# First projection on the input before its norm, modulation slices between projections, decayed keys and queries one head later

## The chip, the cores and the metric

One core of one Trainium2 chip runs the whole program. The time is the device time of that core in microseconds (us); the kernel before takes 1657.59 us, the median of three runs (1657.0 to 1659.45). All arithmetic is in 32-bit floats. TensorE is called PE, VectorE DVE, ScalarE ACT, GpSimd POOL, and the queue that issues the loads SP.

## What is computed

Two transformer blocks on one sequence of 256 tokens with 1024 features. Only the parts that the change touches stand here.

```python
# block 1
h = rms_norm(x, norm_mix_g)          # x * rsqrt(mean(x*x)) * g
u = h @ w_in                         # q, k, v; conv input a, b; state space input
sb, conv, ssm = attention(..), conformer_conv(..), s5_ssm(..)
x = x + branch_norm(concat(sb, conv, ssm)) @ w_out
x = x + memory_cross_attention(rms_norm(x), rms_norm(mem), ..)
x = x + ffn(rms_norm(x))
# block 2
mod   = silu(c) @ w_mod_2 + b_mod_2             # six rows of 1024: shifts, scales, gains
mod_c = silu(c_ctx) @ w_mod_2 + b_mod_2
h, hc = modulated norms of x and ctx
y = mLSTM(h, hc) and gated linear attention(h, hc), then w_out_2
x = x + g1 * y
x = x + g2 * peer_ffn(..)            # 16384 experts, read densely
return rms_norm_2(x, norm_f_g)
```

In gated linear attention the keys and queries are multiplied by exponentials of a running sum of the log decays ("decayed keys", "decayed queries") before the scores `att`.

## The kernel before

Activations lie feature-major: 8 tiles of 128 features by 256 tokens, `x[:, k, :]`. Five engines run five instruction lists, written out by hand; semaphores join them. What stands earlier on an engine's list runs earlier, and a wait on a list holds up all that stands behind it.

**Weights** come in slices of 1 MB into a ring of six slots. PE's list sets the order of the slices (`weights()`), and SP issues the loads in that order (L1178), each when PE has finished with the slice six places before it. One projection (`project`, 16 matmuls of 128x128 by 256 tokens) uses one slice, and so does one step of `mod_items`, which does only four matmuls with a 32-column stationary operand.

**Products** go round four PSUM banks (`begin`), and a bank is written again only after the engine that takes its product has read it. Some later products use four upper banks (`upper=1`).

**Start.** ACT squares x, PE sums the squares over the features (`mix_sum`), ACT takes the square root, DVE the reciprocal (L1255), and DVE then writes h = x * g * r in eight slices (L1278), each released on its own. PE runs three projections from it: "u" (slice 8 of `w_in`), "conv_b" and "conv_a". DVE does a long run of small state space work after h, up to b_ready, then copies u (L1326), subtracts the turns (L1329), takes conv_a (L1333), normalizes the memory tokens and runs the 31 taps of the convolution (L1346). PE waits for the taps later on.

**Modulation.** The product with `w_mod` is cut into 24 slices, eight for each of three rows, which lie between other work. The function `mod_items(n)` does n of them. After eight, ACT copies a row (`mod_row`, L2073), and `mod_turn(r)` turns it on PE. Before the change 4, 2 and 5 slices stand close together just ahead of the first output projection ("mix_out", 0 to 3); seven are earlier, six later. The mixed activations are ready after three norms in a row on DVE (state space, convolution, attention; L1255 and L1457).

**Gated linear attention** lies between the four heads of mLSTM. PE's list is `similarities(0)`, ..., `similarities(3)`, `values(2)`, `values_of("gv", 2)`, the four transposes of the decayed keys and the scores (`gla_keys_and_scores`), `values_of("gv", 3)`, `values(3)`, then the sums "add" and the gates "mo" and "gr". DVE's list, head by head, is `latent_decays(hd+1)` (L1750), `decayed(hd+1)` (L1759), then `quotient(hd)` (L1774 to L1785), and at head 1 `decayed_keys()` (L1729) ahead of the quotient and `decayed_queries()` (L1737 to L1739) behind it. Two bank rules matter: the second product of `similarities(3)` goes to a bank that `quotient(1)` has to clear, and the first of `values(2)` to one that `latent_decays(3)` has to clear.

## Time and profile before

| what | value |
|---|---|
| median of three runs | 1657.59 us |
| the profiled execution | 1655.44 us, span 1652.2 us |
| PE busy | 1585.1 us, 96% of the span |
| PE weight loads busy | 1423.3 us, 86% |
| DVE busy | 1114.6 us, 67% |
| ACT busy | 719.7 us, 44% |
| the chain that ended last | PE 87%, DVE 8%, DMA 3%, ACT 1% |
| mean granted clock of TensorE | 0.98 of full speed |

The span is the time from the first to the last instruction of the profiled execution. All moments below are us from its start. The chain that ended last is followed backwards from the last instruction: a share of an engine in it is time in which nothing else would have let the program end sooner. PE's idle time is what the change can reach; it lies mostly in the first 350 us and between 640 and 790 us. A PE matmul of 32-bit floats shows as two entries, so "x16" is eight matmuls.

### The profile page before, as it was taken

To read this page: it belongs to the slowest core of one execution; us is meant where nothing else is said; L and a number is where in the kernel's file an instruction comes from. 1 tells how busy PE (TensorE), PEld (TensorE's weight loads), DVE (VectorE), ACT (ScalarE), POOL (GpSimd) and SP (SyncE) were. 2 spreads that over 40 slices of the span, in tenths; PEclk is the share of its full clock that TensorE was granted. 3 is DMA by queue.
4 is the path that set the end of the run, shared out by engine and by line. 5 is a ranking of instruction groups with operands and counts; after the bars stand their busy time and mean duration, and the time that the engine had idled before them with its cause. 6 is when DMAs were issued, how large, how long until landed. Compare 5 with 4: busy or idle time off the path is not lost.

```text
span 1652.2 us, 28703 instructions
## 1 busy us (share of the span) xinstructions
PE 1585.1 (96%) x10694; PEld 1423.3 (86%) x10694; DVE 1114.6 (67%) x1943; ACT 719.7 (44%) x1034; POOL 53.8 (3%) x104
## 2 busy tenths in 40 slices
PE   7999899899999999899999999999999999999996
PEld 6677477689999988688999999999999888888885
DVE  6993231347544696675559999898894777777776
ACT  4225201344443456242444565555554544444442
POOL 2001000000000003400000000000000000000000
PEclk9999899999999999999899999999999999999998
DMA  6253834535553323061538887755557777777773
GB/s 264 102 195 131 370 114 178 180 115 188 180 179 104 108 77 103 1 221 62 189 89 229 223 226 226 216 155 161 160 149 223 231 236 237 238 237 236 237 235 103
DMA packets 94400, 293.59 MB, mean 178 GB/s; under 512 B 10480, under 2 KB 43376, under 8 KB 81392
## 3 DMA queue, kind: packets, MB, share of 16 engines
q1 hardware_dynamic: 94176, 292.21, 54.7%
q8 instruction: 57, 0.93, 0.2%
q14 instruction: 23, 0.19, 0.0%
q10 hardware_dynamic: 144, 0.26, 0.0%
HBM read 274.60 MB, written 17.83 MB: 177 GB/s over the span
## 4 chain that ended last, share of the span: by engine, by line
PE 87%; DVE 8%; DMA 3%; ACT 1%; issue 1%; SPq 0%; DVEq 0%; POOL 0%; ACTq 0%
PE ps L428 87%; DMA ring<-in_w_mod 1%; DVE big L1346 1%; DVE split_ring L1880 1%; DVE big L1776 1%; DVE big L1255 1%; DMA ring<-in_peer_u 0%; DVE hh L1556 0%; DVE x L2015 0%; DMA ring<-in_w_mo 0%; DVE big L1929 0%; DVE big L1933 0%; DVE big L1931 0%; DMA ring<-in_w_gv 0%; DMA kept_acts<-par 0%
## 5 line engine op out<-in xcount | busy, mean ns | idle before, releaser
L428 PE MATMUL ps<-split_hh,split_ring 128*128 128x256 f32 x3296 | 410.3, 284 | 3.2 <-DVE split_ring L1880 2.0
L428 PEld LDWEIGHTS ps<-split_hh,split_ring 128*128 128x128 f32 x3296 | 400.4, 192 | 4.6 <-ACT big L2040 1.4
L428 PE MATMUL ps<-split_ring 128*128 128x256 f32 (+1 forms) x2224 | 391.0, 335 | 2.2 <-DVE split_ring L1880 2.1
L428 PEld LDWEIGHTS ps<-split_ring 128*128 128x128 f32 x2224 | 339.1, 188 | 47.6 <-DVE split_ring L1880 2.4
L1880 DVE TENSOR_TENSOR split_ring<-ring,split_ring 128x1024 fp32r<-128x1024 f32 x256 | 311.6, 1219 | 49.5 <-ACT split_ring L2415 46.2
L2422 ACT ACTIVATE split_ring<-ring 128x1024 fp32r<-128x1024 f32 x128 | 135.9, 1062 | 179.2 <-DMA ring<-in_peer_v 179.2
L2415 ACT ACTIVATE split_ring<-ring 128x1024 fp32r<-128x1024 f32 x128 | 135.2, 1057 | 63.4 <-DMA ring<-in_peer_u 63.4
L428 PE MATMUL ps<-split_ffn_h,split_ffn_w 128*128 128x256 f32 x1056 | 130.4, 287 | 3.5 <-ACT split_ffn_h L2236 3.5
L428 PEld LDWEIGHTS ps<-split_ffn_h,split_ffn_w 128*128 128x128 f32 x1056 | 129.3, 194 | 4.6 <-issue 3.9
L1527 DVE TENSOR_TENSOR split_ffn_w<-ring,split_ffn_w 128x2048 fp32r<-128x2048 f32 x33 | 75.6, 2290 | 54.7 <-ACT split_ffn_w L2221 54.7
L428 PE MATMUL ps<-hh,ring 128*128 128x256 f32 x480 | 107.8, 386 | 4.3 <-DVE hh L1278 4.3
L1989 DVE TENSOR_TENSOR split_ring<-ring,split_ring 128x256 fp32r<-128x256 f32 x128 | 54.4, 425 | 84.9 <-ACT split_ring L2429 84.8
L428 PEld LDWEIGHTS ps<-hh,ring 128*128 128x128 f32 x480 | 92.6, 194 | 19.7 <-issue 6.9
L428 PE MATMUL ps<-big 128*128 128x256 f32 (+12 forms) x656 | 88.6, 327 | 14.1 <-DVE big L1750 4.8
L428 PEld LDWEIGHTS ps<-big 128*128 128x128 f32 (+5 forms) x656 | 69.9, 169 | 36.7 <-issue 17.2
L2040 ACT ACTIVATE big<-ps 128x512 f32<-128x512 f32 (+1 forms) x62 | 35.2, 595 | 147.9 <-PE ps L428 124.9
L428 PE MATMUL ps<-big,ring 128*128 128x256 f32 x408 | 92.1, 386 | 0.8 <-DVE big L1515 0.8
L428 PEld LDWEIGHTS ps<-big,ring 128*128 128x128 f32 x408 | 78.5, 194 | 13.4 <-issue 1.4
L1984 DVE TENSOR_TENSOR ring<-ring,big 128x256 f32<-128x256 f32 x128 | 80.3, 628 | 1.5 <-DMA ring<-kept_acts 1.4
L2221 ACT ACTIVATE split_ffn_w<-ring 128x2048 fp32r<-128x2048 f32 x33 | 63.0, 1909 | 32.3 <-PE ps L428 32.3
L1963 DVE TENSOR_SCALAR ring<-tables,idx 128x128 f32<-128x128 f32 x256 | 71.1, 341 | 6.2 <-PE ps L428 6.2
L428 PE MATMUL ps<-split_hid_high,split_ffn_w 128*128 128x256 f32 x352 | 63.5, 283 | 0.0
(312 smaller groups left out, 1779.4 us busy)
## 6 DMA issues: line engine op xcount, KB each, us to landing
ring<-in_peer_u SPq DMA_DIRECT2D x128, 512.0 KB, 3.9
ring<-in_peer_v SPq DMA_DIRECT2D x128, 512.0 KB, 3.6
ring<-in_w_mod SPq DMA_DIRECT2D x24, 1024.0 KB, 5.2
ring<-in_ffn_in SPq DMA_DIRECT2D x22, 1024.0 KB, 4.9
ring<-kept_acts SPq DMA_DIRECT2D x128, 128.0 KB, 3.4
ring<-in_ffn_out SPq DMA_DIRECT2D x11, 1024.0 KB, 4.9
ring<-in_w_out SPq DMA_DIRECT2D x8, 1024.0 KB, 11.8
ring<-in_peer_wq SPq DMA_DIRECT2D x8, 1024.0 KB, 6.4
```

What stands on the lines that cost most here:

```text
L428: return nc.tensor.matmul(out, lhsT, rhs, start=start, stop=stop, skip_group_check=True)
L1255: link(v.reciprocal(r, r))
L1346: ins = v.scalar_tensor_tensor(conv[:, a, :], src, w, conv[:, a, :], ALU.mult, ALU.add)
L1527: v.tensor_tensor(fw_low[:, q, :], ring[:, (ffn_at + n) % RING, :], fw_high[:, q, :].bitcast(F32), ALU.subtract).then_inc(flag("ffn_weight ...
L1880: v.tensor_tensor(low[:, q, :], tile[:, q, :], high[q].bitcast(F32), ALU.subtract)\
L1963: v.tensor_scalar(hot[n % 4][:, q, 0, :], iota, idx[:, 0, at:at + 1], idx[:, 2, at:at + 1], ALU.is_equal, ALU.mult)
L1984: v.tensor_tensor(weighted_[:, q, :], act_in[:, q, :], g_, ALU.mult).then_inc(flag("whole_weighted"), 1)
L1989: v.tensor_tensor(w_low[:, q, :], weighted_[:, q, :], w_high[:, q, :].bitcast(F32), ALU.subtract).then_inc(e_ready, 1)
L2040: s.took(key, a_(dst, bank if src is None else src(bank), ACT.Copy, scale=scale))
L2221: a_(fw_high[:, n % 3, :], ring[:, at % RING, :], ACT.Copy).then_inc(flag("ffn_weights_high"), 1)
L2415: a_(u_high[q], u_tile[:, q, :], ACT.Copy).then_inc(flag("u_high_ready"), 1)
L2422: a_(v_high[q], v_tile[:, q, :], ACT.Copy).then_inc(flag("v_high_ready"), 1)
```

## The change

It has three parts.

1. **First projection.** DVE writes xg = x * g in eight slices while the sum of squares is still being taken, and PE projects "u" from xg. The factor r, which is one number for each token, is multiplied in when DVE takes the product. The slices of h are written as before, and "conv_b" is now the first to use them.
2. **Modulation slices.** The groups of 4, 2 and 5 ahead of "mix_out" become 2 and 2. Of the other seven, three follow the first three projections of "mix_out", one stands ahead of the first projection of "xq", two follow its first two and one follows its sums. The second turn moves to that last place, and ACT's copy of the second row goes between its takings of "xq".
3. **Decayed keys and queries.** On DVE they move from head 1 to head 2, together with the low half of weight half 21. On PE the fourth block of values, "gv" 3, goes between the transposes of the keys and the scores, and ACT copies it out ahead of the scores.

```diff
@@ tensor
-            project("u", ("dve",), "w_in", 8, arriving("h_mix"))
-            project("conv_b", ("act",), "w_in", 7, hk)
+            def scaled(k):
+                pe.wait_ge(flag("x_scaled"), k + 1)
+                return xg[:, k, :]
+            project("u", ("dve",), "w_in", 8, scaled)
+            project("conv_b", ("act",), "w_in", 7, arriving("h_mix"))
...
-            mod_items(4)
             weighted(3)
             mod_items(2)
-            mod_turn(0)
             pe.wait_ge(flag("branch_squares_ready"), 3)
             total("sb_sum", [sq[:, i, :] for i in range(4)])
-            mod_items(5)
-            mod_turn(1)
+            mod_items(2)
+            mod_turn(0)
             pe.wait_ge(flag("mixed_ready"), 3)
             for i in range(4):
                 project(("mix_out", i), ("dve",), "w_out", i, lambda k: mixed[:, k, :])
+                if i < 3:
+                    mod_items(1)
...
+            mod_items(1)
             arrived = arriving("h_xa")
             for i in range(4):
                 project(("xq", i), ("act",), "xa_wq", i, arrived)
+                if i < 2:
+                    mod_items(1)
             pe.wait_ge(flag("squares_ready"), 4)
             sums_of_heads("xq_sum")
+            mod_items(1)
+            mod_turn(1)
             inverses_of_heads("xq", 0)
...
             values_of("gv", 2, wv, 1)
-            gla_keys_and_scores()
+            gla_keys()
             values_of("gv", 3, wv, 1)
             release_half(*wv)
+            gla_scores()
             values(3)
@@ vector
-            r = reciprocal_std("mix_sum")
-            for i in range(4):
-                s.wait(f"x_loaded{i}", 16)
+            for k in range(KD):
+                s.wait(f"x_loaded{k // 2}", 16)
+                v.tensor_scalar(xg[:, k, :], x[:, k, :], col("mix_g", k), None, ALU.mult).then_inc(flag("x_scaled"), 1)
+            mix_r = r = reciprocal_std("mix_sum")
...
-            s.took("u", v.tensor_copy(u.rearrange("p a t -> p (a t)"), bank))
+            s.took("u", v.tensor_tensor(u, bank.rearrange("p (a t) -> p a t", a=2),
+                                        mix_r.unsqueeze(1).broadcast_to([P, 2, T]), ALU.mult))
...
-                if hd == 1:
+                if hd == 2:
                     decayed_keys()
                 quotient(hd)
-                if hd == 1:
+                if hd == 2:
                     decayed_queries()
                     half_low(21)
@@ scalar
             squares(sq, xk).then_inc(flag("squares_ready"), 1)
-            mod_row(1)
...
             for i in range(4):
                 heads_raw("xq", i, xq)
+                if i == 2:
+                    mod_row(1)
...
+            copy_out(("gv", 3), gv[:, 3, :])
             s.wait("att_zeroed")
...
-            copy_out(("gv", 3), gv[:, 3, :])
```

The buffer of xg is that of `mixed`, which is written only much later.

**PE around the modulation slices.** A row with `ps<-ring,big 32x512` is the slices (x4 is one slice), `128x8` a turn, `big,ones` a sum over features, and `big,ring 128x256` the "mix_out" projections (x16 is one). Before:

```order
L428 MATMUL ps<-big,ones 128x256 x4
L428 MATMUL ps<-ring,big 32x512 x16
L428 MATMUL ps<-big 64x256
L428 MATMUL ps<-big 64x128
L428 MATMUL ps<-big 64x256
L428 MATMUL ps<-big 64x128
L428 MATMUL ps<-ring,big 32x512 x8
L428 MATMUL ps<-big 128x8 x4
L428 MATMUL ps<-big,ones 128x256 x4
L428 MATMUL ps<-ring,big 32x512 x20
L428 MATMUL ps<-big 128x8 x4
L428 MATMUL ps<-big,ring 128x256 x32
```

The same place in the changed kernel, from the last attention pair on:

```order
L429 MATMUL ps<-ring,big 32x512 x8
L429 MATMUL ps<-big,ones 128x256 x4
L429 MATMUL ps<-ring,big 32x512 x8
L429 MATMUL ps<-big 128x8 x4
L429 MATMUL ps<-big,ring 128x256 x16
L429 MATMUL ps<-ring,big 32x512 x4
L429 MATMUL ps<-big,ring 128x256 x16
L429 MATMUL ps<-ring,big 32x512 x4
L429 MATMUL ps<-big,ones 32x256 x8
L429 MATMUL ps<-big,ring 128x256 x16
L429 MATMUL ps<-ring,big 32x512 x4
```

Four slices stand ahead of the first output projection in place of eleven, and one behind each of the first three.

**DVE at heads 1 and 2 of gated linear attention.** Before, from the end of `decayed(2)`: the keys are L1729, the quotient of head 1 L1774 to L1785, the queries begin with L1737.

```order
L1759 SCALAR_TENSOR_TENSOR big<-ps,big 128x256
L1729 TENSOR_TENSOR big<-big 128x1024 x2
L1774 SCALAR_TENSOR_TENSOR big<-ps,big 128x256
L1775 TENSOR_TENSOR big<-big,ps 128x256
L1776 RECIPROCAL big<-big 128x256
L1778 TENSOR_TENSOR big<-ps,big 128x256
L1774 SCALAR_TENSOR_TENSOR big<-ps,big 128x256
L1775 TENSOR_TENSOR big<-big,ps 128x256
L1776 RECIPROCAL big<-big 128x256
L1782 TENSOR_TENSOR big<-ps,big 128x256
L1785 TENSOR_TENSOR big<-big 128x256
L1737 TENSOR_TENSOR big<-big 128x512
```

In the changed kernel, from the end of the quotient of head 1 (L1801): L1766 is `latent_decays(3)`, L1775 `decayed(3)`, and L1745 the keys.

```order
L1798 TENSOR_TENSOR big<-ps,big 128x256
L1801 TENSOR_TENSOR big<-big 128x256
L1766 TENSOR_SCALAR big<-ps,big 128x256
L1766 TENSOR_SCALAR big<-ps,big 128x128 x2
L1766 TENSOR_SCALAR big<-ps,big 128x256
L1775 SCALAR_TENSOR_TENSOR big<-ps,big 128x512 x2
L1775 SCALAR_TENSOR_TENSOR big<-ps,big 128x256
L1775 SCALAR_TENSOR_TENSOR big<-ps,big 128x128 x2
L1775 SCALAR_TENSOR_TENSOR big<-ps,big 128x256
L1745 TENSOR_TENSOR big<-big 128x1024 x2
```

The quotient of head 1 now follows `decayed(2)` directly, and the decays of head 3 follow it, ahead of the keys.

## Rows read from the trace of the kernel before

**Rows 1.** The page: the chain that ended last, by engine

```profile
PE 87%; DVE 8%; DMA 3%; ACT 1%; issue 1%; SPq 0%; DVEq 0%; POOL 0%; ACTq 0%
```

**Rows 2.** The timeline of the start (start us, duration us, engine, line, operation, count [idle before, releaser])

```profile
5.76 6.34 PE L428 MATMUL ps<-big,ones 128*128 128x256 f32 x16 [5.76 <-ACT big L2031]
...
7.14 0.70 DVE L1272 MEMSET big<- 128x768 f32 x1
...
15.78 3.26 DVE L1278 SCALAR_TENSOR_TENSOR hh<-x,par,big 128x256 f32<-128x256 f32 x8
...
16.41 16.50 PE L428 MATMUL ps<-hh,ring 128*128 128x256 f32 x64 [4.31 <-DVE hh L1278]
...
32.84 4.49 DVE L1329 TENSOR_TENSOR big<-big 128x2048 f32<-128x2048 f32 x2
...
36.20 7.07 PE L428 MATMUL ps<-hh,ring 128*128 128x256 f32 x32
...
43.38 0.69 DVE L1333 TENSOR_TENSOR big<-ps,big 128x512 f32<-128x512 f32 x1 [6.04 <-PE ps L428]
```

**Rows 3.** DMA issues between 3.1 and 3.5 us: count, size, us to landing

```profile
ring<-in_w_in SPq DMA_DIRECT2D x1, 1024.0 KB, 7.6
```

**Rows 4.** Windows: us, busy PE, PEld, DVE, ACT, POOL (x instructions), PEclk, DMA share, GB/s

```profile
16.40:20.00 3.60, 3.59 (x9) 2.88 (x10) 3.43 (x13) 3.57 (x7) 0.00 (x0) 0.50 1.01 423
282.00:286.00 4.00, 4.00 (x10) 3.11 (x11) 1.89 (x5) 0.00 (x0) 0.00 (x0) 0.50 0.43 180
```

**Rows 5.** Waits of PE for the slices: us in total, times, longest

```profile
PE ps L428 <- DMA ring<-in_w_mod: 6.9, 7, 1.4
```

**Rows 6.** The timeline, 170 to 200 us: slices, norms, first output projection

```profile
173.10 2.78 PE L428 MATMUL ps<-ring,big 128*32 128x512 f32 x24
...
174.79 1.75 DVE L1255 RECIPROCAL big<-big 128x256 f32<-128x256 f32 x1 [3.70 <-ACT big L2036]
...
176.12 1.07 PE L428 MATMUL ps<-ring,big 128*32 128x512 f32 x8 [0.24 <-DMA ring<-in_w_mod]
...
187.37 1.67 DVE L1457 SCALAR_TENSOR_TENSOR big<-big,par 128x256 f32<-128x256 f32 x4
...
192.22 1.94 PE L428 MATMUL ps<-ring,big 128*32 128x512 f32 x8 [1.44 <-DMA ring<-in_w_mod]
...
198.29 16.02 PE L428 MATMUL ps<-big,ring 128*128 128x256 f32 x64
```

**Rows 7.** The timeline after the "xq" projections

```profile
281.95 3.78 PE L428 MATMUL ps<-big,tables 128*128 128x256 f32 x8 [2.41 <-DVE big L1469]
```

**Rows 8.** DVE, 664 to 684 us

```profile
665.03 3.20 DVE L1729 TENSOR_TENSOR big<-big 128x1024 f32<-128x1024 f32 x2
...
674.80 0.68 DVE L1737 TENSOR_TENSOR big<-big 128x512 f32<-128x512 f32 x1
...
678.41 1.21 DVE L1596 TENSOR_TENSOR split_ring<-ring,split_ring 128x1024 fp32r<-128x1024 f32 x1
...
682.33 2.34 DVE L1759 SCALAR_TENSOR_TENSOR big<-ps,big 128x512 f32<-128x512 f32 x6 [1.40 <-POOL big L2576]
```

**Rows 9.** ACT, exponentials of head 3 (second direction)

```profile
675.28 0.83 ACT L2321 ACTIVATE big<-ps,big 128x256 f32<-128x256 f32 x2
```

**Rows 10.** PE, 674 to 716 us

```profile
674.48 1.13 PE L428 MATMUL ps<-big 128*128 128x256 f32 x4 [1.81 <-DVE big L1782]
680.43 3.29 PE L428 MATMUL ps<-big 128*128 128x256 f32 x8 [4.82 <-DVE big L1750]
...
693.27 2.69 PE L428 MATMUL ps<-big 64*64 64x64 f32 x64
...
701.46 1.68 PE L428 MATMUL ps<-big 128*128 128x256 f32 x8
...
705.45 1.59 PE L428 MATMUL ps<-big 64*64 64x128 f32 x32
...
715.36 1.09 PE L428 MATMUL ps<-big 64*64 64x128 f32 x16 [1.34 <-DVE big L1782]
```

More of the change, by code:

```diff
@@ L197, in program @@
         mixed = area.take(8, T)
+        xg = mixed
         mod_rows = area.take(2, 512)
@@ L917, in values, with gla_keys @@
                     last.then_inc(made, 1)
-            def gla_keys_and_scores():
+            def gla_keys():
                 pe.wait_ge(flag("gla_ready"), 1)
@@ L926, in gla_keys_and_scores, with gla_scores @@
                     last.then_inc(made, 1)
+            def gla_scores():
                 pe.wait_ge(flag("gla_ready"), 2)
```

## The prediction

> **What bounds the kernel now.** I read the chain that ended last first: 87% of the span is PE and only 8% DVE and 3% DMA [rows 1]. So the end moves only where PE idles or runs at the low clock, and the first question for each part is how much of either lies at its place. Then I read the timeline at the three places the change touches, with the granted clock of TensorE from the windows. A change within 0.2% (3.3 us) is about what a measurement of this kernel cannot tell from none.
>
> At the start PE ends the sum of squares at 5.76 + 6.34 = 12.1 us and then waits 4.31 us for the first slice of h [rows 2]. The clock is 0.50 of full speed, the 1.2 GHz level, when PE comes back [rows 4]. The next 64 entries take 16.50 us, where 32 entries of the same kind take 7.07 us later, so 64 at full speed take 14.1 and 2.4 us are lost.
>
> Ahead of "mix_out" PE waits seven times for slices, 6.9 us in total [rows 5]. The slices cost 2.78 us for 24 entries, 0.93 us each, and 1.94 us at the low clock [rows 6]. "mix_out" starts at 198.29, 9 us after the last norm is ready (187.37 + 1.67 = 189.0), and its first 64 entries take 16.02 in place of 14.1 us. After "xq" PE waits 2.41 us for a reciprocal and then runs at the low clock again [rows 4, 7].
>
> In gated linear attention PE waits 1.81, 4.82 and 1.34 us for DVE, and the eight entries after the second wait take 3.29 us, where the same eight take 1.68 us later [rows 10].
>
> **Part 1, the first projection.** DVE is free at 7.14 + 0.70 = 7.84. Eight slices of xg at 0.41 us, the price of a slice of h (3.26 for eight), are done at 11.2 [rows 2]. A simpler operation may be cheaper; either way they end before 12.1 and before the square root that the reciprocal needs, so they cost nothing. The weights were issued at 3.1 and landed 7.6 us later, 10.7 [rows 3]. So "u" starts at 12.1 with no gap behind the sum, and I take full speed. "u" ends at 19.2; h is complete at 15.78 + 3.26 = 19.0, so "conv_b" has no wait. It ends at 26.3. The memory sum (36.20 - 32.91 = 3.3) and "conv_a" (7.07) end at 36.7. DVE, whose list up to there is not moved, is done with the turns at 32.84 + 4.49 = 37.3 [rows 2]. It then takes "conv_a" at 37.4 and not at 43.38: **6.0 us** earlier. The taps hang on that and PE waits for the taps, so 6.0 is what counts, not the 6.7 that PE gains. Taking "u" is now a product with r; the like operation on "conv_a" from PSUM takes 0.69 us [rows 2] and lies ahead of b_t on PE by several us. If only the wait goes and not the clock loss, the gain is 4.3.
>
> **Part 2, the slices.** Times here are on the old axis. The last attention pair goes first, 0.9 us from 173.1, then two slices to 175.9, the attention sum 0.9 and two slices to about 178.8; the fourth slice of this place landed by 176.12 in the old order [rows 6], so none waits. With the turn (0.9) PE is through at 179.8. The norms are DVE's: from 174.79 it does three reciprocals of 1.75 and eight products (0.42 each from 1.67 for four) [rows 6], 8.7 us in all, so the mixed activations are ready at 183.5. "mix_out" starts there and not at 198.29: 14.8 us. PE now has a new wait of 3.7 us. Behind it come six slices (5.6 us) that were ahead of it, and the 1.9 us at the low clock in "mix_out" may go: 14.8 + 1.9 - 5.6 = 11.1. The seventh slice and the second turn (1.9 us) fill the wait of 2.41 us after "xq" [rows 7] and cost nothing; without that wait they would cost 1.9. What was half speed behind it (4.00 us busy in 282 to 286 at 0.50 [rows 4], and 1.2 us more) costs 2.6 us that I take as saved. Against it stands the new wait of 3.7 us, of a length with the 4.31 us after which the clock was low at the start; I charge 2.0 us in "mix_out", near the 1.9 and 2.4 us lost there in the rows, with 0 and 3.4 as ends. Part 2 gives **11.7 us**, with 6 and 13.7 as ends. SP: each moved slice issues one load of 1 MB. Before, eleven came with next to no PE work between them; now 1 MB of slice and 1 MB of weights go with 8 us of PE work, and in the saturated stretch of the start (423 GB/s [rows 4]) 2 MB take 5 us. ACT's copy of the second row (0.6 us) lies between two takings that are 7 us apart.
>
> The Trainium skill (TensorE: Matmul & The Clock Gate, Part 1) says that the throttled state is the default, that activity releases it, and that the cold stretch of one and the same kernel differs from run to run, so one should not fit to a particular cold count. The trace agrees with the first two (0.50 after the idle time, full speed later). By the third, the clock's part of my sum should be left out; that is a rival below.
>
> **Part 3, keys and queries.** DVE ends `decayed(2)` at 665.03. It spent 3.2 us on the keys, 6.6 on the quotient (to 674.80) and 3.6 on the queries (to 678.41) [rows 8]. Now the quotient comes first and ends at 671.7. The second product of `similarities(3)` loses its 1.81 us wait and runs until 673.6. ACT's exponentials for the second direction (about 1.1 us with its copy, 0.83 in [rows 9]) and 0.7 us of decays put the banks free at about 673.8, the first one a microsecond sooner. `values(2)` starts at 673.6 and not at 680.43: 6.8 us; with no idle time the clock stays up, 1.3 more: 8.1. Now the other side: DVE goes on with a wait of 1.40 and 2.3 for `decayed(3)` [rows 8] to 677.5, keys to 680.6, quotient to 687.3, queries to 690.9. PE needs the keys for the transposes, which begin some 2 us ahead of 693.27 - 8.1 = 685.2, so they are early. It needs the queries behind "gv" 3, which has come forward: 685.2 + 5.6 = 690.8, where 5.6 is the stretch from the end of the scores (693.27 + 2.69) to 701.46 [rows 10]. They come with a wait of 0 to 0.3. What follows is unchanged, so "add" starts at 697.6 and not at 705.45. The 1.34 us wait at 715.36 goes too: it hung on the quotient of head 3, which waits for weight halves that load when "gv" 3 is made, and that is now some 10.7 us earlier (690.8 and not 701.46). Part 3 gives 7.8 + 1.3 = **9.1 us**. The half that DVE splits later, 21, is needed by "mo" behind the first "add", at 699; it is split at 692.
>
> **Sum.** 6.0 + 11.7 + 9.1 = 26.8 us. The profiled execution took 1655.44 us, so 1628.6 for one like it; it lies 2.15 us below the median of 1657.59. For the median: **1630.8 us**.
>
> **Rivals.**
> - *The clock gives nothing back.* Waits alone: 4.3 in part 1; 6.9 less the new 3.7 to 4.0 and plus the 1.9 hidden, 4.8, in part 2; 1.81 + 4.82 + 1.34 - 0.2, so 7.8, in part 3. Sum 16.9: 1640.7 us. For it speaks that the low stretches move when work moves; against it, that each in the rows follows an idle time which the change removes. This is also the time by the page's third rule. Chance 0.15.
> - *The queries come late.* They are last on DVE and the margin is nil. If the masks or ACT hold up `decayed(3)` by 5 us, every microsecond goes to PE: 1635.8 us. Chance 0.10.
> - *Part 1 is half lost:* a slice of xg or the weights come late, or the low stretch comes in "conv_a" instead. 3 us less: 1633.8. Chance 0.06.
> - *Slower.* A load is issued when the slice six places earlier is released. With a slice between any two projections those six places hold only some 17 us of work in "mix_out" (two projections and three slices) where six projections held 42. Loads here land after 7.6 us [rows 3], so they are in time; from 17 us on each microsecond of landing is a wait at each of the loads of "w_out" and "xa_wq". Landings of 23 us or more at five of them eat 30 us: 1661 us. Chance 0.03; that the two sides cancel, 0.01.
>
> **How the numbers follow.** The forecast has 0.65. Its own range is 1627 to 1634: 2.0 better if the new wait does not lower the clock, 3 worse if part 2's credits fail. The range of 1625 to 1642 takes in the first three rivals and a little of what measured medians differ by, and leaves out the slower one and some misjudged sizes. Faster by over 0.2%: 0.65 + 0.15 + 0.10 + 0.06 = 0.96. Within 0.2%: 0.01. Slower: 0.03.
>
> **What would show it.** Part 1: PE's entries run on from 12.1 with no gap, no PEclk of 0.50 near 16, and DVE takes "conv_a" at 37.4. Part 2: no wait on w_mod, one wait of 3.7 us on DVE's norm product ahead of "mix_out", "mix_out" at 183.5 - 6.0 = 177.5. Part 3: no wait of 4.82 on the latent decays, and the scores wait on the queries by less than 0.5 us. A wait of several microseconds on the queries, on w_out or on the taps would prove me wrong.

## The result, and the profile after

The changed kernel takes 1633.87 us, the median of six runs (1628.71 to 1637.98), beside 1658.35 us for six runs of the kernel before. The ratio is 0.985, with a 95% interval of 0.983 to 0.987. That is 24.5 us less, where 26.8 were forecast. The forecast of 1630.8 us was 3 us low; the range of 1625 to 1642 holds the time. The traced execution took 1637.16 us with a span of 1634.0, so it was one of the longer ones; the mean granted clock of TensorE rose from 0.98 to 0.987.

The page of the changed kernel, busy time and the chain that ended last by engine (it answers to [rows 1]):

```profile
PE 1582.2 (97%) x10694; PEld 1417.9 (87%) x10694; DVE 1116.6 (68%) x1951; ACT 719.0 (44%) x1034; POOL 53.9 (3%) x104
...
PE 87%; DVE 9%; DMA 2%; ACT 1%; issue 1%; SPq 0%; DVEq 0%; POOL 0%; ACTq 0%; POOLq 0%
```

DMA went from 3% to 2% of the chain and DVE from 8% to 9%: the waits for slices are gone, and DVE is what PE waits for in their place.

**Part 1.** The timeline of the start, PE first and then two rows of DVE (it answers to [rows 2]):

```profile
5.89 5.80 PE L429 MATMUL ps<-big,ones 128*128 128x256 f32 x16 [5.89 <-ACT big L2047]
11.54 7.07 PE L429 MATMUL ps<-big,ring 128*128 128x256 f32 x32
18.44 7.07 PE L429 MATMUL ps<-hh,ring 128*128 128x256 f32 x32
25.35 3.62 PE L429 MATMUL ps<-big,ones 128*128 128x256 f32 x16
...
8.00 2.06 DVE L1290 TENSOR_SCALAR big<-x,par 128x256 f32<-128x256 f32 x8
...
36.74 0.69 DVE L1349 TENSOR_TENSOR big<-ps,big 128x512 f32<-128x512 f32 x1
```

The eight slices of xg take 2.06 us, 0.26 each, not the 0.41 of a slice of h. "u" follows the sum with no gap, both projections run at 7.07 us for 32 entries, and DVE takes "conv_a" at 36.74 in place of 43.38, 6.64 us earlier. Then PE comes to the mean over the taps, which DVE makes, and to the query/key sum behind it. The timeline of before, then that of the changed kernel:

```profile
73.73 1.13 PE L428 MATMUL ps<-big,ones 128*128 128x256 f32 x4 [2.44 <-DVE big L1346]
...
96.98 1.07 PE L428 MATMUL ps<-big 128*32 128x256 f32 x16 [1.41 <-ACT big L2097]
```

```profile
67.08 2.07 PE L429 MATMUL ps<-big,ones 128*128 128x256 f32 x4 [4.84 <-DVE big L1362]
68.95 22.21 PE L429 MATMUL ps<-hh,ring 128*128 128x256 f32 x96
92.56 1.07 PE L429 MATMUL ps<-big 128*32 128x256 f32 x16 [1.41 <-ACT big L2113]
```

The taps come 6.65 us earlier, but PE waits 4.84 us for them and not 2.44. Behind the longer wait four entries take 2.07 us in place of 1.13 and the next 96 take 22.21 in place of 20.88. So only 4.42 us are left at the query/key sum. The granted clock shows why (windows of the changed kernel; PEclk is the third figure from the end of a row):

```profile
62.00:68.00 6.00, 1.16 (x4) 0.83 (x3) 6.00 (x14) 1.09 (x2) 0.00 (x0) 0.73 0.57 217
67.00:72.00 5.00, 4.92 (x13) 3.97 (x14) 4.93 (x4) 0.00 (x0) 0.00 (x0) 0.54 0.00 0
179.00:183.00 4.00, 3.96 (x9) 3.19 (x10) 0.00 (x0) 0.00 (x0) 0.00 (x0) 0.50 1.03 426
282.00:286.00 4.00, 3.44 (x25) 1.38 (x23) 1.54 (x5) 1.55 (x5) 0.00 (x0) 1.00 0.63 219
```

**Part 2.** The first two rows above are the taps, the wait and what follows it; the third is the start of "mix_out", at 0.50, the 1.2 GHz level; the fourth is a stretch that was at 0.50 in [rows 4] and is now at full speed. The timeline from the norms to "xq" and behind it (it answers to [rows 6] and [rows 7]):

```profile
179.04 9.73 PE L429 MATMUL ps<-big,ring 128*128 128x256 f32 x32 [2.77 <-DVE big L1473]
188.70 1.06 PE L429 MATMUL ps<-ring,big 128*32 128x512 f32 x8
...
234.96 7.17 PE L429 MATMUL ps<-hh,ring 128*128 128x256 f32 x32
242.07 1.06 PE L429 MATMUL ps<-ring,big 128*32 128x512 f32 x8
243.06 7.17 PE L429 MATMUL ps<-hh,ring 128*128 128x256 f32 x32
...
267.54 1.06 PE L429 MATMUL ps<-ring,big 128*32 128x512 f32 x8
268.54 1.06 PE L429 MATMUL ps<-big 128*128 128x8 f32 x8
270.15 1.99 PE L429 MATMUL ps<-big,tables 128*128 128x256 f32 x8 [0.56 <-DVE big L1485]
...
336.41 2.08 PE L429 MATMUL ps<-split_ffn_h,split_ffn_w 128*128 128x256 f32 x5 [3.51 <-ACT split_ffn_h L2253]
```

No wait of PE for a slice is left. "mix_out" starts at 179.04. The place ahead of part 2 comes 4.43 us earlier than before, so part 2 alone moved it by 198.29 - 4.43 - 179.04 = 14.82 us. Its wait for the norms is 2.77 us, and its first 32 entries take 9.73 us, 2.66 over 7.07. The wait of 2.41 after "xq" has shrunk to 0.56.

**Part 3.** DVE, and then PE, in the last heads of gated linear attention (they answer to [rows 8] and [rows 10]):

```profile
661.67 3.21 DVE L1745 TENSOR_TENSOR big<-big 128x1024 f32<-128x1024 f32 x2
...
674.46 0.68 DVE L1755 TENSOR_TENSOR big<-big 128x512 f32<-128x512 f32 x1
```

```profile
655.70 3.51 PE L429 MATMUL ps<-big 128*128 128x256 f32 x16
...
675.20 4.40 PE L429 MATMUL ps<-big 64*64 64x64 f32 x72 [0.94 <-DVE big L1755]
...
681.92 1.59 PE L429 MATMUL ps<-big 64*64 64x128 f32 x32
```

Sixteen entries in 3.51 us, with no wait in front or between, stand where the waits of 1.81 and 4.82 us and the low clock stood. The scores wait 0.94 us for the queries. "add" starts at 681.92 and not at 705.45.

**The stages of the two traces.** Gain of the changed kernel in us, from the starts of the same work in both:

| from | to | before | after | gain |
|---|---|---|---|---|
| 0 | query/key sum | 96.98 | 92.56 | 4.42 |
| query/key sum | FFN (350.44, 336.41) | 253.46 | 243.85 | 9.61 |
| FFN | "add" (705.45, 681.92) | 355.01 | 345.51 | 9.50 |
| "add" | last stage (1275.82, 1249.03) | 570.37 | 567.11 | 3.26 |
| last stage | end of the span | 376.4 | 385.0 | -8.6 |

These are differences of one trace each, and two of them mislead; the traces taken later, at the end of the next section, put them right. Of the 3.26 us, 1.93 lie ahead of a wait of 4.07 us for ACT (at 761.17, where it was 786.63): the 1.34 of part 3 are among them. The other 1.33 lie behind that wait, where the low clock was shorter (0.66 in place of 0.52 over the 10 us from there); the forecast had nothing for it. The last row was not foreseen at all: the change touches nothing there.

### The profile page after: what moved, and what is told of

Its sections match the earlier page's. It is cut to its first block, busy times and chain, and to the rows that moved or that the text cites. A ratio compares the mean times of both kernels' runs of the same rounds, so it can differ in the third digit from the quotient of the medians.

```text
span 1634.0 us, 28710 instructions
## 1 busy us (share of the span) xinstructions
PE 1582.2 (97%) x10694; PEld 1417.9 (87%) x10694; DVE 1116.6 (68%) x1951; ACT 719.0 (44%) x1034; POOL 53.9 (3%) x104
## 4 chain that ended last, share of the span: by engine, by line
PE 87%; DVE 9%; DMA 2%; ACT 1%; issue 1%; SPq 0%; DVEq 0%; POOL 0%; ACTq 0%; POOLq 0%
PE ps L429 87%; DVE big L1362 1%; DVE big L1269 1%; DVE split_ring L1896 1%; DMA ring<-in_peer_u 1%; DVE hh L1572 0%; DVE x L2031 0%; DVE big L1792 0%; DVE big L1945 0%; DVE big L1949 0%; DMA kept_acts<-acts 0%; DVE big L1947 0%; ACT split_ring L2432 0%; DMA ring<-in_w_gv 0%; DMA ring<-in_peer_v 0%
## 5 line engine op out<-in xcount | busy, mean ns | idle before, releaser
L429 PE MATMUL ps<-split_ring 128*128 128x256 f32 (+1 forms) x2224 | 399.4, 340 | 2.1 <-DVE split_ring L1896 2.1
L429 PE MATMUL ps<-big,ring 128*128 128x256 f32 x440 | 100.1, 387 | 3.5 <-DVE big L1473 2.8
L429 PEld LDWEIGHTS ps<-big,ring 128*128 128x128 f32 x440 | 84.9, 194 | 18.1 <-DVE big L1473 2.9
L429 PE MATMUL ps<-hh,ring 128*128 128x256 f32 x448 | 100.3, 384 | 0.0
L429 PEld LDWEIGHTS ps<-hh,ring 128*128 128x128 f32 x448 | 85.7, 192 | 16.0 <-issue 4.2
L429 PE MATMUL ps<-big 128*128 128x256 f32 (+12 forms) x656 | 84.7, 321 | 6.8 <-ACT big L2056 3.7
```

The lines of the kernel that those rows point to most:

```text
L429: return nc.tensor.matmul(out, lhsT, rhs, start=start, stop=stop, skip_group_check=True)
```

## The experiments

Runs named together were made on one chip beside the same runs of the kernel before.

**One part at a time, and the change once more.** `p1_only`, `p2_only` and `p3_only` are the kernel before with the hunks of one part of the change; `after_again` is the changed kernel. Their edits, cut to a line or two for each:

```diff
p1_only
-            project("u", ("dve",), "w_in", 8, arriving("h_mix"))
+            project("u", ("dve",), "w_in", 8, scaled)
p2_only
-            mod_items(5)
-            mod_turn(1)
+            mod_items(2)
+            mod_turn(0)
...
+                if i < 3:
+                    mod_items(1)
p3_only
-                if hd == 1:
+                if hd == 2:
                     decayed_keys()
```

> The kernel before with only the first part of the change (first projection on the unnormed input, scaled on the way out). Theory A, from the two traces: TensorE gains about 6.6 us up to conv_a, runs ahead of VectorE, waits longer at the taps (4.8 us where it waited 2.4), and the clock is low for some 6 us after that wait, so only 4.4 us are left at the query/key sum (at 92.6 us instead of 97.0) and 4.0 to 4.8 us at the end. Theory B, as predicted: 6.0 us reach the end, and the query/key sum comes at 91. Theory C: the last stage (add_experts, with the values out of the ring) takes 355 us in some executions and 363 us in others, whatever the kernel; then the times of this kernel fall into two groups some 7 us apart or all into one, and the stage's length in the trace goes with the time. If the length of that stage were caused by the change as a whole, it would be 355 here.

> The kernel before with only the second part (modulation slices spread between more projections). Theory A, from the two traces: mix_out starts 14.8 us earlier counted from this part's first change, its wait for mixed grows to 2.8 us, mix_out runs 2.7 us longer on the low clock after that wait, the remaining slices take back 5.6, the low clock after the first query projection goes (2.6), and the FFN begins 9.6 us earlier than before (340.8 instead of 350.4); with the low clock at the end of the FFN gone too (1.4) 11.0 us in all, 9.5 to 11.5. Theory B, as predicted: 11.7 us. Theory C: no low clock is given back after the query projection; then 7 to 8 us.

> The kernel before with only the third part (decayed keys and queries one head on). Theory A, from the two traces: the three waits around each head's values and scores fall to 0.4 and 0.9 us, and the first projection of mo starts 9.8 us earlier than before; 1.2 us more come from a shorter low clock in the FFN behind it; 9.0 to 11.0 us in all. Theory B, as predicted: 9.1 us. If the longer last stage (363 instead of 355 us) comes from this part, the total gain is only 1 to 3 us and the trace shows 363 there.

> The changed kernel once more. Theory A: the length of the last stage differs between executions of one kernel: the times fall into two groups, near 1630 and near 1637, and the profiled execution shows a stage of 355 us if it belongs to the first and 363 us if it belongs to the second. Theory B: the longer last stage is caused by the change: it is 363 us whatever the execution's time, and the two groups come from another place.

| kernel | median us, runs | ratio to before, 95% interval | gain, us | forecast |
|---|---|---|---|---|
| before | 1659.46, 17 | | | |
| p1_only | 1654.66, 12 | 0.9971, 0.9956 to 0.9985 | 4.8 | 6.0 |
| p2_only | 1648.17, 6 | 0.9931, 0.9913 to 0.995 | 11.3 | 11.7 |
| p3_only | 1650.57, 6 | 0.9946, 0.9929 to 0.9963 | 8.9 | 9.1 |
| after_again | 1634.54, 5 | 0.9844, 0.9827 to 0.9862 | 24.9 | 26.8 |

The three gains add up to 25.0 us, and the change gives 24.9. So there is no sign that the parts touch one another, though each gain is known to some 3 us only. Part 1 gives less than forecast, as theory A has it, though its interval (2.5 to 7.3 us) still holds 6.0. Parts 2 and 3 cannot be told from the forecast by their times. Theory C of `p2_only` (7 to 8 us) lies below its interval of 8.3 to 14.4. No times fell into two groups, as theory C of `p1_only` and theory A of `after_again` had it: those of `p1_only` lie anywhere between 1648.16 and 1659.67, those of `after_again` between 1631.36 and 1638.15.

The traces say more than the times. The query/key sum stands at 92.58 in `p1_only`, at 92.56 in the first trace of the changed kernel, and at 90.52 in the second. The second, from the wait at the taps on:

```profile
67.26 1.13 PE L429 MATMUL ps<-big,ones 128*128 128x256 f32 x4 [3.16 <-DVE big L1362]
68.23 20.88 PE L429 MATMUL ps<-hh,ring 128*128 128x256 f32 x96
90.52 1.07 PE L429 MATMUL ps<-big 128*32 128x256 f32 x16 [1.41 <-ACT big L2113]
```

The taps come at the same time as in the first trace. But here the low clock fell 20 us earlier, where DVE was the later of the two anyway: nine entries had taken 4.13 us from 41.33 in the first trace, four took 3.68 us from 41.50 in this one. PE came to the taps later, waited 3.16 and not 4.84 us, and kept the clock. At the query/key sum 6.46 us were gained. Six traces of this study are of kernels with part 1 and the wait at the taps. In four the wait was 4.83 to 4.85 us, and the four entries behind it took 1.69 to 2.08 us every time, the sum standing at 91.05 to 92.58. In two it was 3.16 and 3.15 us, the entries took 1.13, and the sum stood at 90.52 and 91.09. At 41 us the low clock cost PE 1.7 us (15.70 in place of 14.00 for the 32 entries there) and the sum nothing; at 67 it cost both 2.2. What it costs depends on whether it falls under another engine's work.

Nor does it take part 1 to bring it to the taps. `p3_only` has the start of the kernel before, and in its trace the 32 entries at 46.91 took 14.00 us, where they took 15.49 to 15.68 in the five other traces with that start. PE came to the taps early, waited 4.09 us, and then ran at 0.58:

```profile
71.91 2.08 PE L428 MATMUL ps<-big,ones 128*128 128x256 f32 x4 [4.09 <-DVE big L1349]
73.78 22.46 PE L428 MATMUL ps<-hh,ring 128*128 128x256 f32 x96
97.65 1.07 PE L428 MATMUL ps<-big 128*32 128x256 f32 x16 [1.41 <-ACT big L2100]
```

In the other five the wait was 2.41 to 2.44 us and the clock stayed up. Over all six traces with the old start the sum stands at 95.34 to 97.65, 96.70 in the mean; over the six with part 1 at 91.67. That is 5.0 us for part 1, by many traces in place of one pair.

`p3_only` shows part 3 alone: from the FFN (348.04) to the first projection behind "add" (696.74) 348.70 us, where the first trace of before has 706.97 - 350.44 = 356.53. That is 7.83 us, and 7.8 were forecast for this place. In the changed kernel itself the stage gave another amount in each trace, as shown at the end of this section.

**Covering the new waits.** `taps` takes the mean over the taps behind the second query/key projection; `fill` puts one slice more ahead of the turn and one behind it, both ahead of the wait for the norms; `best` has both, and the queries of part 3 ahead of the quotient.

```diff
taps, best
-                if i == 0:
+                if i == 1:
                     conv_mean()
fill, best
-            mod_items(2)
+            mod_items(3)
             mod_turn(0)
+            mod_items(1)
             pe.wait_ge(flag("mixed_ready"), 3)
...
-                if i < 3:
+                if i < 1:
                     mod_items(1)
best
                     decayed_keys()
+                    decayed_queries()
                 quotient(hd)
                 if hd == 2:
-                    decayed_queries()
```

> The changed kernel with the mean over the convolution's taps taken behind the second query/key projection instead of ahead of it, so that 7 us of matmuls lie under TensorE's wait for VectorE's last tap (4.84 us in one trace of the changed kernel, 3.16 in the other). Theory A (TensorE's wait is what part 1 of the change now ends in, and the clock falls behind it in some executions): no wait and no low clock there in any trace, the query/key sum at 88 to 90.5 us where it was at 92.56 and 90.52, and 1.5 to 4 us off the end. Theory B (VectorE is what bounds this stretch): the later mean makes its normalisation late by 2 us and TensorE waits as long at the query/key sum or the ssm output; no change within 0.5 us, or up to 2 us slower.

> The changed kernel with one modulation item more and the turn ahead of mix_out's wait for mixed, and fewer slices between mix_out's projections. Theory A (the wait of 2.77 us before mix_out is free time, and the low clock behind it costs 2.66 us more in some executions): the item of 1.9 us is taken in by the wait, mix_out runs at 7.07 us for 32 matmuls, and 1.9 to 4.5 us are gained at the FFN (336.41 and 333.50 in the two traces). Theory B: the weights of the item have not landed by then, and TensorE waits for them as long as it waited for mixed; no change.

> The changed kernel with three edits: the mean over the taps behind the second query/key projection, the modulation items ahead of mix_out's wait, and the decayed queries of the next head ahead of the quotient of this one on VectorE, which should take away the wait of 0.94 us before each head's scores (0.9 us in all). Theory A: the three add up, 4.5 to 9 us faster than the changed kernel, near 1627 us where that one is near 1634. Theory B (what is taken away comes back as the next wait): within 2 us of it.

| kernel | median us, runs | ratio to before (1658.18, 9 runs), 95% interval |
|---|---|---|
| taps | 1632.97, 5 | 0.983, 0.9805 to 0.9854 |
| fill | 1632.29, 5 | 0.9834, 0.981 to 0.9857 |
| best | 1626.17, 5 | 0.9791, 0.9765 to 0.9818 |

`best` beats both kernels: 32.0 us less than before, and 8.4 less than the changed kernel's 1634.54 in the runs above, at the upper end of what theory A gave. The two were not run side by side, but their ratios to before, 0.9765 to 0.9818 and 0.9827 to 0.9862, do not overlap. One at a time, the first two cannot be told from the changed kernel by their times, and the traces must say what they did. `taps`, PE:

```profile
54.74 13.98 PE L429 MATMUL ps<-hh,ring 128*128 128x256 f32 x64
68.56 1.03 PE L429 MATMUL ps<-big,ones 128*128 128x256 f32 x4
69.42 13.98 PE L429 MATMUL ps<-hh,ring 128*128 128x256 f32 x64
84.81 1.07 PE L429 MATMUL ps<-big 128*32 128x256 f32 x16 [1.41 <-ACT big L2113]
...
108.07 2.81 PE L429 MATMUL ps<-big,tables 128*64 128x256 f32 x24 [0.78 <-DVE big L1399]
112.28 1.08 PE L429 MATMUL ps<-big,tables 128*64 128x256 f32 x8 [1.40 <-DVE big L1408]
113.80 2.09 PE L429 MATMUL ps<-big 64*128 64x256 f32 x16 [0.44 <-DVE big L1417]
```

The wait and the low clock behind it are gone, and the query/key sum comes at 84.81, 5.7 us before the better trace of the changed kernel and well below the 88 that was expected. Only a part of the 5.7 us is the wait: the low clock at 41 us, there in that trace, is absent here too (14.00 us for the 32 entries). But three waits for DVE, 2.6 us together, stand at 108 to 114, where that trace has none: DVE's chain through the state space is next. "mix_out" starts at 174.45, 2.55 us before the 177.00 of that trace. Both theories hold half: TensorE's wait was the end of part 1, and VectorE takes over after 3 us. The trace of `best`, with the same edit, has no low clock up to the query/key sum either (84.49).

`fill`, PE at "mix_out":

```profile
178.71 7.14 PE L429 MATMUL ps<-big,ring 128*128 128x256 f32 x32 [0.97 <-DVE big L1474]
```

The wait is 0.97 and not 2.77 us, and the 32 entries take 7.14 and not 9.73 us. From here to the FFN (333.11) it is 154.40 us, against 157.37 in the first trace of the changed kernel and 156.50 in the second: 2.1 to 3.0 us gained, inside theory A's range. More was gained at first: from the start of "mix_out" to the work behind its third projection it was 4.55 us against the first trace. But a low clock now stood at a place where no trace of the changed kernel has one, and took 1.7 us back:

```profile
292.95 3.68 PE L429 MATMUL ps<-big 128*128 128x256 f32 x8 [0.75 <-ACT big L2057]
```

The eight entries take 1.99 us in the changed kernel behind the same wait of 0.75 us. `best` has it too, with 3.41.

`best` in the last heads:

```profile
666.28 4.40 PE L429 MATMUL ps<-big 64*64 64x64 f32 x72
```

The scores start without a wait, 337.83 us after the FFN (328.45), where it was 675.20 - 336.41 = 338.79: 0.96 us for the 0.94 of the wait. These two traces can be set side by side, for neither met a low clock between 345 us and the scores; the two later ones of the changed kernel took 340.24 and 340.46. So a part of the 8.4 us of `best` may be that its executions met fewer low clocks by chance, and no run tells how much. Its wait ahead of "mix_out" is 1.12 us, and the trace puts it down to a load of `w_out`; the last norm product of DVE ended 0.26 us ahead of its end, so the loads are nearly the limit there.

**The last stage.** In the first traces wide matmuls (512 columns) took 391 ns in the kernel before and 399 in each kernel with a part of the change. `before_again`, `before_third` and `before_fourth` are the kernel before, `after_third` the changed one, each traced once; `pairs` issues the same matmuls in another order. In this stage a matmul is one entry and not two.

```diff
pairs, add_experts
-                for m in LAST_SUMS:
-                    mm(ps[:, m, :], v_high[q][:, e], w_parts[:, q, :], first_, False)
-                    last = mm(ps[:, m, 0:T], v_low[:, q, e], w_high[:, q, :], False, False)
+                for n in range(0, KD, 2):
+                    two = LAST_SUMS[n:n + 2]
+                    for m in two:
+                        mm(ps[:, m, :], v_high[q][:, e], w_parts[:, q, :], first_, False)
+                    for m in two:
+                        last = mm(ps[:, m, 0:T], v_low[:, q, e], w_high[:, q, :], False, False)
```

> The kernel before once more, for its trace. All five traces with any part of the change show the last stage (add_experts with the values out of the ring) at the slower rate: 285 matmuls per 50 us, 399 ns for each of 512 columns, 384 us from its first matmul to the end of the span; the one trace of before shows 290 to 291, 391 ns and 376 us. Theory A: the rate is drawn anew in each execution, whatever the kernel; this trace may then show 285 and 399 ns, and would by itself prove it. Theory B: any of the three parts brings the slower rate; then this trace shows 290 and 391 ns again.

> The kernel before a third time, for its trace. The last stage (add_experts) ran at 391 ns a wide matmul in the first trace of before, at 391 for its first 150 us and at 399 from then on in the second, and at 399 throughout in all eight traces of kernels with a part of the change. Theory A: the rate is drawn in each execution, whatever the kernel; the third trace may show either, and 399 from the start would prove it. Theory B: the change brings 399, and before starts the stage at 391 each time.

> The kernel before a fourth time, for its trace: the same two theories as for the third. If both show 391 ns at the stage's start, the change (any part of it) costs up to 8 us there; if either shows 399, it doesn't.

> The changed kernel a third time, for its trace. Theory A: 391 or 399 ns a wide matmul in the last stage, and a total of 1629 to 1631 us if it is 391. Theory B: 399 ns, as in the other two. On the start of the program: the low clock behind the taps wait, there in one of two traces, comes or not, and the query/key sum stands near 92.5 us or near 90.5.

> The changed kernel with the matmuls of the last stage in another order: both wide ones (512 columns) of two banks, then both narrow ones (256 columns), where wide and narrow alternate. Theory A (the two rates are two repeating patterns in which TensorE's matmuls follow each other, 116 and 228 ns apart by turns or a longer pattern with 240 ns in it, and depend on the order they are issued in): the mean of a pair moves from 345 or 353 ns to another value, by more than 3 ns either way, and the stage's length with it (2048 pairs, so 6 us for 3 ns). Theory B (what slows the stage lies outside TensorE, in the transfers or the splits beside it): 353 ns a pair and 363 us as in the other traces of the changed kernel.

Windows of 50 us, PE busy and its count first, PEclk third from the end. The first trace of before:

```profile
1300.00:1350.00 50.00, 50.00 (x290) 44.10 (x289) 38.20 (x55) 25.28 (x38) 0.00 (x0) 1.00 0.75 237
...
1450.00:1500.00 50.00, 50.00 (x290) 44.08 (x289) 37.94 (x54) 24.55 (x36) 0.00 (x0) 1.00 0.75 238
```

The second (`before_again`) and the fourth (`before_fourth`):

```profile
1300.00:1350.00 50.00, 50.00 (x290) 43.72 (x290) 38.27 (x55) 24.60 (x36) 0.00 (x0) 1.00 0.76 236
...
1450.00:1500.00 50.00, 50.00 (x285) 43.23 (x284) 37.38 (x54) 23.83 (x35) 0.00 (x0) 1.00 0.76 229
```

```profile
1300.00:1350.00 50.00, 50.00 (x285) 43.36 (x285) 37.50 (x54) 23.54 (x36) 0.00 (x0) 1.00 0.73 233
```

The changed kernel's third trace:

```profile
1300.00:1350.00 50.00, 50.00 (x290) 43.56 (x289) 37.18 (x53) 24.59 (x36) 0.00 (x0) 1.00 0.76 235
1350.00:1450.00 100.00, 100.00 (x568) 86.74 (x567) 75.68 (x108) 48.43 (x72) 0.00 (x0) 1.00 0.74 231
```

By the trace PE is 100% busy at a clock of 1.00 in every one of them (the ends of matmuls are modelled there, so this isn't PE at its peak), and yet it starts 290 matmuls in some windows and 285 in others, in one and the same execution. `before_third` has 285 from the start as well. So theory A holds: the rate differs between executions and within one, and 285 needs no part of the change. Whether both kernels meet it equally often is not shown: at 1300 to 1350 us two of four traces of before had 290, and one of the nine that have a part of the change and the old order. The stage's length, from its first matmul to the end of the span, was 376.4, 382.1, 383.7 and 383.5 us in the four traces of before and 385.0, 384.6 and 382.5 in the three of the changed kernel. The first trace of before, from which the forecast was made, was the exception, and the loss of 8.6 us in the table above is in the main that. By the means, 381.4 and 384.0, there are 2.6 us between the kernels, less than the 7.3 among the traces of before alone.

`pairs` takes 1629.49 us (4 runs; ratio 0.9817, 0.9798 to 0.9837, beside a median of 1661.36), and its window has another count:

```profile
1350.00:1450.00 100.00, 100.00 (x577) 87.25 (x576) 75.71 (x109) 49.20 (x72) 0.00 (x0) 1.00 0.75 236
```

577 for 100 us is 347 ns a pair, where a count of 290 in 50 us makes 345 and 285 makes 351, and the stage takes 1626.4 - 1246.55 = 379.9 us. Its windows of 50 us from 1300 to 1550 us have 289 each, and those of no other trace have. That speaks for theory A: the order in which TensorE gets the wide and narrow matmuls has a part in the rate. But it moved 4 to 5 ns from the slower rate and only 2 from the better one, less than the 3 that were expected, and one trace doesn't show that this order never meets the slower rate. The stage is 2.6 to 5.1 us shorter than in the three traces of the changed kernel, but 1.5 shorter than in those of `fill` and `best` (381.4 in both). By the times, the interval of `pairs` overlaps that of the changed kernel (0.9827 to 0.9862). (The expectation counted 2048 pairs; there are 128 blocks of experts times 8 banks, 1024, so 3 ns a pair are 3 us.) The order and the edits of `best` were not run together. What makes an execution leave the rate of 290 was not found: it goes over with PE busy all the time (`after_third` began at the better rate and took 1636.55 us, not the 1629 to 1631 that were expected of such an execution), and I saw no way back in any trace.

**All traces of the two kernels.** The stages again, in us, in the order in which the traces were taken:

| stage | before | changed | means | gain |
|---|---|---|---|---|
| 0 to query/key sum | 96.98, 96.51, 96.87, 95.34 | 92.56, 90.52, 91.09 | 96.4, 91.4 | 5.0 |
| to FFN | 253.46, 253.30, 253.47, 250.22 | 243.85, 242.98, 242.97 | 252.6, 243.3 | 9.3 |
| to "add" | 355.01, 354.88, 355.00, 354.91 | 345.51, 348.63, 348.85 | 355.0, 347.7 | 7.3 |
| to last stage | 570.37, 571.60, 570.84, 570.91 | 567.11, 567.96, 567.68 | 570.9, 567.6 | 3.3 |
| last stage | 376.4, 382.1, 383.7, 383.5 | 385.0, 384.6, 382.5 | 381.4, 384.0 | -2.6 |

Up to the last stage the means differ by 25.0 us, the 24.9 of the times. Beside the start, two stages differ within one kernel, and each time the low clock is what differs. "mix_out" of the kernel before took 16.00 to 16.06 us for its first 64 entries in the first three traces; in the fourth the clock was back up before it began, and the stage is 3.2 us shorter:

```profile
195.50 14.05 PE L428 MATMUL ps<-big,ring 128*128 128x256 f32 x64
```

And the 9.50 us up to "add" in the first table are the best case. In the first trace of the changed kernel the eight entries behind a wait of 0.99 us at 549 took 1.22 us; in the two others, as in all traces of before and in `p3_only`, they took 2.08. And the scores, behind the new wait for the queries, took 5.94 and 5.87 us for 72 entries in these two, where the first had 4.40:

```profile
673.74 5.94 PE L429 MATMUL ps<-big 64*64 64x64 f32 x72 [0.95 <-DVE big L1755]
```

The granted clock is 0.73 from 673.7 to 679.7 us. The wait of 0.94 us is short, and still a low clock followed it in three of the seven traces that have it (`fill` is the third, with 6.02). There the part took 1.5 us back, which none of the first traces showed.

## Why the prediction was right

The direction, the places and the order of sizes were right: PE's idle time and low clock at three places, one after the other on the path. Each part gave a little less than its forecast (4.8, 11.3 and 8.9 us by the times for 6.0, 11.7 and 9.1). What was forecast and what was measured, by the steps of the prediction:

- *"u" starts behind the sum with no gap.* Right, at 11.54 for 12.1, since the sum ran 0.5 us faster in this trace (11.71 and 12.29 in the two others). It ran at full clock in all three. DVE took "conv_a" at 36.74 for 37.4.
- *"PE waits for the taps, so 6.0 is what counts, not the 6.7 that PE gains."* This step fell short, by 1.2 us in the times and 1.0 in the means of the traces. DVE's list did come forward by 6.65 us at the taps, but the sum left out what a longer wait of PE may do to the clock behind it. In four of six traces the wait was 4.83 to 4.85 us, a low clock followed, and in the changed kernel's first one 4.4 us were left. In its two others the forecast was about met (6.46 and 5.89 us against the first trace of before).
- *"mix_out" starts 14.8 us earlier.* 14.82 between the first traces, with a wait of 2.77 us for 3.7. That it fits so closely is luck with the base: counted from the sums ahead of part 2, "mix_out" began after 27.0 to 27.1 us in three traces of before, after 26.0 in the fourth, and after 12.3 in all three of the changed kernel.
- *The slices cost 5.6 us behind it.* Too low, by 1.1 us. From the start of "mix_out" to "xq" the stretch grew by (234.96 - 179.04) - (249.25 - 198.29) = 4.96 us, and within "xq" by 2.49. Less the difference of the two low clocks in "mix_out" (2.66 - 1.92), six slices took 6.7 us, 1.1 each. The 0.93 came from three slices in a row [rows 6]. A single slice between two projections costs more: 243.06 - 234.96 = 8.10 us for a projection with one, and 6.9 us for one without.
- *2.0 us for a low clock in "mix_out", and 1.9 saved there.* 2.66 in the first trace, 1.8 in the two others of the changed kernel (8.86 us for 32 entries). It did follow the new wait in five of the six traces that have it (in `pairs` the 32 entries took 7.17 us behind a wait of 2.77), and in `fill`, where the wait was 0.97 us, it was gone. The 1.9 were there to be saved in three of the four traces of before.
- *The wait of 2.41 us takes in a slice and a turn, and the low clock behind it goes.* Right: 0.56 us of wait are left, 282 to 286 is at 1.00, and the stretch up to the projections behind it gave 2.24 us for the 2.6 forecast. All four traces of before had the low clock there and none of the three of the changed kernel.
- *Part 3, 7.8 us at "add".* 7.83 in `p3_only`; 8.9 for the whole part by the times, for 9.1. The margin of the queries was 0.94 us short, where 0 to 0.3 was forecast and 0.5 was named as the limit, and a low clock behind that wait took another 1.5 us in two of the changed kernel's three traces. The forecast had neither this nor the 1.3 us gained behind the wait for ACT at 761 us. That the two are of one size is luck.

The Trainium skill (TensorE: Matmul & The Clock Gate, Part 1) was quoted with a rule that the cold stretch differs from run to run. The traces bear it out: the low clock at the start of the program came at one of two places in the changed kernel. But the rival that was built on it, that the clock gives nothing back (16.9 us), fell: 24.9 us came. At the start the place of a low clock varied between 41 and 67 us. Behind "xq" it was fixed: the kernel before had it in four traces of four, and the changed kernel, without that wait, in none of three. So a single trace can mislead by 1 to 3 us at a stage, in either direction.

The base, the median and not the trace alone, was well chosen. The traced execution of before had a last stage some 7 us shorter than the three traced later and was the lowest of them in time; from its 1655.44 us alone the forecast would have been 1628.6, another 2.2 us too low.

## What to carry to other kernels

When a gain on one engine ends in a wait for another, ask what the longer wait does to the clock behind it, and put independent work under it at once: the change and the covering of its three new waits gave 32 us, of which some 8 came from a few moved lines. Then look where the low clock went, for it can turn up behind another wait. Price a moved piece in the company it will have, not in a row of its like. And trace a kernel more than once before a stage's difference of 2% is given a cause.

## What was not expected of the hardware

- TensorE at full clock and 100% busy by the trace ran the same stream of matmuls at two rates, 290 or 285 in 50 us (391 or 399 ns for the wide ones), held each for 50 us and more, and went from the better to the worse inside an execution. Over the stage it is up to 8 us. With the places of the low clock (4.9 us up to the last stage among the four traces of before) it is large enough for the spread of 8 to 12 us between runs of one kernel, though no run tells how much of the spread is its own. With wide and narrow in twos one trace had a third rate, 347 ns a pair.
- A low clock of TensorE cost the program nothing at 41 us and 2 us at 67, since at 41 VectorE was the later engine.
- A low clock followed a wait of 0.94 us in three traces of seven, and did not follow one of 2.77 us in one of six. In these traces the length of the one wait doesn't tell what follows.
- VectorE's product of x (fp32, 128x256, from and to SBUF) with a factor for each partition took 0.26 us, where the product that takes r, a second tensor, as well takes 0.41 (each an eighth of a run of eight). The Trainium skill (VectorE: DVE Perf Modes, the perf-mode tier table) puts this operation at twice the rate of a product of tensors for fp32 in SBUF; the trace agrees in the direction, with a factor of 1.6 at this size, but the slower operation here is a product with a factor and a tensor in one (scalar_tensor_tensor), for which that table has no row.
